# Layer 1's retention projection four columns ahead of the softmax attention instead of two

## The reference, cut to what matters

```python
pc = jnp.split(uc @ w_in, splits, axis=-1)
pl = jnp.split(ul @ w_in, splits, axis=-1)
...
b_c, b_l = _retention_branch(pc[1], pl[1], log_decay_raw, ret_norm_g, cos, sin, need_ctx)
c_c, c_l = _gqa_branch(pc[2], pl[2], qk_norm_g, cos, sin, need_ctx)
...
def _attend(q, k, v):
    s = jnp.einsum("bqkgd,bskd->bkgqs", q, k).astype(jnp.float32) * HEAD_DIM ** -0.5
    p = jax.nn.softmax(s, axis=-1).astype(v.dtype)
    return jnp.einsum("bkgqs,bskd->bqkgd", p, v)
```

## Time and profile before

| | before |
|---|---|
| median of 3 runs | 2147.62 us (2146.8 to 2147.97) |
| the profiled execution, its own time | 2146.09 us |
| span of its trace | 2144.2 us |
| PE busy | 2074.1 us, 97% of the span |
| DVE busy | 1568.4 us, 73% |
| ACT busy | 1150.0 us, 54% |
| POOL busy | 144.0 us, 7% |
| layer 1's retention columns and attention | from 1046.4 to 1109.0 us of the span |

### The profile page before, as it was taken

One profiled execution on the slowest core, in us unless ns is written; L12 is line 12 of the kernel. 1 busy time (PEld: TensorE's weight loads), 2 busy tenths in 40 slices (PEclk: granted clock), 3 DMA queues, 4 the chain that ended last, 5 costly groups with the idle time before them and its releaser, 6 DMA issues. The chain is left out here.

```text
span 2144.2 us, 36008 instructions
## 1 busy us (share of the span) xinstructions
PE 2074.1 (97%) x14750; PEld 1719.1 (80%) x14750; DVE 1568.4 (73%) x2201; ACT 1150.0 (54%) x1581; POOL 144.0 (7%) x118
## 2 busy tenths in 40 slices
PE   8999899999999999998998999999999999999997
PEld 5887687888888888877776899788888888888886
DVE  4546665889567555446466666699999999999998
ACT  4253443333432222244544355588888888888886
POOL 0013520000000000000045100100000000000000
PEclk9999999999999999999999999999999999999999
DMA  6700034454154545413000554599999999999995
GB/s 265 271 18 2 3 121 157 177 216 177 59 221 186 207 183 195 172 62 118 21 1 4 218 190 145 206 388 379 380 375 372 394 378 383 378 376 382 375 418 199
DMA packets 68485, 470.11 MB, mean 219 GB/s; under 512 B 7712, under 2 KB 8672, under 8 KB 14048
## 3 DMA queue, kind: packets, MB, share of 16 engines
q1 hardware_dynamic: 62464, 441.62, 53.5%
q10 hardware_dynamic: 4704, 21.98, 2.6%
q0 software_dynamic: 1152, 4.19, 0.5%
HBM read 455.15 MB, written 12.62 MB: 218 GB/s over the span
## 5 line engine op out<-in xcount | busy, mean ns | idle before, releaser
L2441 DVE TENSOR_TENSOR wsp_l<-ring,wsp_h 128x1024 fp32r<-128x1024 f32 x528 | 643.1, 1223 | 48.9 <-ACT wsp_h L1551 14.0
L1551 ACT CAST wsp_h<-ring 128x1024 fp32r<-128x1024 f32 x528 | 555.2, 1054 | 137.1 <-PE bank L719 81.2
L717 PE MATMUL bank<-wsp_h,xTs_h 128*128 128x512 f32 x704 | 283.7, 403 | 0.4 <-DVE wsp_l L2441 0.4
L719 PE MATMUL bank<-wsp_h,xTs_l 128*128 128x512 f32 x704 | 275.6, 391 | 0.0
L718 PE MATMUL bank<-wsp_l,xTs_h 128*128 128x512 f32 x704 | 274.4, 390 | 0.0
L2071 ACT CAST dsp_h<-ring 128x1024 fp32r<-128x1024 f32 x66 | 69.2, 1048 | 244.4 <-PE bank L1427 172.8
L3038 DVE TENSOR_TENSOR dsp_l<-ring,dsp_h 128x1024 fp32r<-128x1024 f32 x66 | 80.9, 1225 | 145.6 <-ACT dsp_h L2071 145.2
L1318 PE MATMUL bank<-u_hi,gsp_h 128*128 128x512 f32 (+1 forms) x512 | 174.1, 340 | 0.0
L1318 PE MATMUL bank<-u_hi,gsp_l 128*128 128x512 f32 (+1 forms) x512 | 172.1, 336 | 0.0
L1318 PE MATMUL bank<-x_lo,gsp_h 128*128 128x512 f32 (+1 forms) x512 | 172.0, 336 | 0.0
L2347 DVE SCALAR_TENSOR_TENSOR products<-ring,cond_rows 128x1024 bf16<-128x1024 f32 x128 | 156.4, 1222 | 5.0 <-DVE dsp_l L3038 0.5
(11 more groups left out here) (399 smaller groups left out, 4106.1 us busy)
## 6 DMA issues: line engine op xcount, KB each, us to landing
ring<-in_moe_tiles_dram SPq DMA_DIRECT2D x264, 1024.0 KB, 7.1
ring<-in_ada_tiles_dram SPq DMA_DIRECT2D x48, 1024.0 KB, 4.8
ring<-in_ffn_tiles_dram SPq DMA_DIRECT2D x33, 1024.0 KB, 6.8
ring<-in_gate_tiles_dram SPq DMA_DIRECT2D x32, 1024.0 KB, 6.8
ring<-in_in_tiles_dram SPq DMA_DIRECT2D x22, 1024.0 KB, 4.8
arena<-in_branch_tiles_dram ACTq DMA_DIRECT2D x8, 1024.0 KB, 7.4
ring<-in_out_tiles_dram SPq DMA_DIRECT2D x8, 1024.0 KB, 4.8
x_rows<-arena SPq DMA_DIRECT2D x1, 3584.0 KB, 15.9
```

The source lines that it names most:

```text
L717: pe.matmul(o, xTs[0][:, kk, :], whi[:, k, :], start=(kk == 0), stop=False)
L719: mm = pe.matmul(o, xTs[1][:, kk, :], whi[:, k, :], start=False, stop=(kk == KD - 1))
L1551: act.copy(wsp[0][:, g % 4, :], half_slot(MOE0, g)).then_inc(s.gq_o.up, 1)
L2441: v.tensor_tensor(wsp[1][:, g % 4, :], half_slot(MOE0, g), wsp[0][:, g % 4, :], ALU.subtract).then_inc(s.gq_pt.up, 1)
```

## The change

In layer 1 four columns stand ahead of the attention instead of two (`AHEAD`), as in layer 0. Column g is thus projected in step g-4 instead of g-2, and steps 8 and 9 have none. So that the weights are split in time, halves 16 and 17 are split before the transposes of the attention (ACT: around `root` and `fourier_out`; DVE: within its normalisation), halves 18 and 19 in the steps 0 and 1 (before: 1 and 2), halves 20 and 21 in the steps 3 and 4 (before: 5 and 6). The copies of PSUM follow the columns, and the copy after the loop is gone since its columns are now copied in step 7. Layer 0 is as it was.

```diff
-AHEAD = (4, 2)
+AHEAD = (4, 4)
...
                 ahead = AHEAD[l]
+                if l:
+                    weight_high(16)
                 root(small[:, 32:56], s.gq_sq, s.gq_rs)
                 fourier_out(0)
                 fourier_out(1)
-                weight_high(16)
+                if l == 0:
+                    weight_high(16)
+                else:
+                    weight_high(17)
...
-                weight_high(17)
+                if l == 0:
+                    weight_high(17)
...
-                    if n in (1, 2):
+                    if n in (1 - l, 2 - l):
                         act.wait_ge(*s.win_mm(UNITS + RDONE[l][0]))
-                        weight_high(17 + n)
+                        weight_high(17 + l + n)
                     if n % 2 and ahead + n < len(RCOLS[l]):
                         retention_evac((ahead + n) // 2)
-                    if n in (5, 6):
+                    if n in (5 - 2 * l, 6 - 2 * l):
                         act.wait_ge(*s.win_mm(UNITS + RDONE[l][1]))
-                        weight_high(15 + n)
+                        weight_high(15 + 2 * l + n)
...
                 else:
-                    retention_evac(RUNITS[l] - 1)
                     for t in range(NT):
                         rt_turn(t, t)
...
                 for t in (0, 2):
+                    if l:
+                        weight_low(16 + t // 2)
                     h0 = 0 if t in tiles else 4
...
                 v.wait_ge(*s.gq_tp(NT))
-                weight_low(16)
-                weight_low(17)
                 if l == 0:
+                    weight_low(16)
+                    weight_low(17)
                     v.wait_ge(*nil_out(32))
...
-                    if n in (1, 2):
-                        weight_low(17 + n)
-                    if n in (5, 6):
-                        weight_low(15 + n)
+                    if n in (1 - l, 2 - l):
+                        weight_low(17 + l + n)
+                    if n in (5 - 2 * l, 6 - 2 * l):
+                        weight_low(15 + 2 * l + n)
                     if n in (3, 4, 7, 8):
```

## The result

| | before | changed |
|---|---|---|
| median of 22 runs each | 2148.04 us | 2153.8 us |
| lowest and highest | 2144.64 to 2151.69 | 2146.3 to 2161.54 |
| ratio, 95% interval | | 1.0023, 1.0015 to 1.0031 |
| the profiled execution, its own time | 2146.09 us | 2161.54 us |

The medians differ by 5.8 us; the ratio of the runs, 1.0023, is 4.9 us, with 3.2 to 6.7 in its interval. The profiled execution of the changed kernel is its slowest run, so it shows more than the typical loss. Of the 15.5 us between the two profiled executions, 3.45 have been lost when column 0 begins (1049.85 instead of 1046.40), ahead of everything that the change can reach: the clock happened to fall in other places there.

The account below looks back on a forecast made before the run. PE, busy 97% of the span, was taken as the bound: +3.65 start, -3.1 clock, +3.7 stall, -1.2 tail make +3.0, plus 1.5 and 1.5 for low clock give +6.0, 2153.6 us; forecast 2151.5 to 2156, range 2148.2 to 2158.

Parts of the forecast that it names:

- The start: Ahead of layer 1's loop: two more columns hide the rotation's 2.82 us wait; scores of head 0 come 3.65 us later.
- The 3.1 us saved in the steps: Steps 0 to 7 without stalls: 40.3 us instead of 43.4, the difference being the price of the low clock.
- The stall in step 3: Late split and rotary step beside POOL in step 3 delay head 4's maximum; PE waits 3.7 us in step 5.
- The clock after the first gap: Low clock behind the 3.7 us idle stretch on PE: 1.5 us, between 0 and 3.1.
- The end: Steps 8 and 9, without columns: last rotary step still ends 7.4 us after step 7's column; PE idle 5.1 us.
- the tail: End of the loop: columns 10 and 11 and their copy no longer stand there, -1.2 us.
- The clock after the second gap: Low clock behind the 5.1 us idle stretch ahead of the retention's transposes: 1.5 us, between 0 and 3.1.
- the rival of a held clock: Rival: the stall in step 3 comes but the clock holds; +3.0 us, 2150.6 us, chance 0.15.
- Nothing behind absorbed the shift: After the retention's transposes: one chain to the program's end, no transfer or other engine absorbing a shift.

Follow-up runs that it names:

- the casts first: The changed kernel with ACT's casts of halves 20 and 21 ahead of the copy of PSUM in layer 1's steps 3 and 4; 2144.99 us, ratio 0.9997.
- changed_again: The changed kernel, nothing altered, run again on the other chip beside the kernel before; 2156.03 us against 2149.16, ratio 1.0036.

## Why the prediction came true, and where two errors cancelled

**The start** held: scores of head 0 predicted 3.65 us later, measured 14.06 - 10.55 = 3.51; the wait for the rotation gone, the clock at 1.00 up to step 5. The 3.1 us saved in the steps held as a sum too, but the prediction called all of it the price of the low clock. PE's wait of 1.08 us for the split of half 17, seen in the profile of idle products in the kernel before, lay hidden in it, and the change removes that wait as well, since the split now stands earlier.

**The stall in step 3** held in size and mechanism: predicted 3.7 us by copy, cast, split and a rotary step behind POOL's three instructions, measured 3.54. The casts first and the run without POOL's tables each took one link of the chain away, and the gap went in both. Filled with idle products, both waits kept their length.

**The clock after the first gap** was put at 1.5 us, from 0 to 3.1. Step 5, scores to scores, took 11.4 us: 5.3 + 3.54 + 2.6 for the clock; in the second profile 11.0, so 2.1. The term was a little too low. The low stretch is 6.8 us long in both; it begins 1.0 us before PE has work again in the first and 2.0 us before it in the second.

**The end** is the term that was mis-sized. I kept the 7.4 us from step 7's column to the end of the last rotary step. It took 1115.33 - 1110.43 = 4.9. The rotary step now starts 0.22 us ahead of POOL's first instruction, where before it started 0.40 after it, and its sixth instruction slips in at 1115.05, as POOL's long third starts at 1115.06. Before, its fifth was caught by the third, by the timeline of DVE:

```profile
1105.20 2.37 DVE L2399 TENSOR_TENSOR arena<-arena 128x128 f32<-128x128 f32 x1
```

That wait, some 2.1 us of these 2.37, was not there, and the whole rotary step took 3.2 us instead of 5.1. The working had seen that the two starts lie within some tenths of each other in step 3, but took over the old length for the end without asking which came first. The rotary step also started sooner after the column, 1.7 us instead of 2.3, since DVE was no longer behind. That POOL is met at all still costs 1.8 us against the 1.4 of a rotary step alone; some 1.2 us of the gap would stand without it (an estimate from these lengths). Predicted were -1.2 for the tail and a gap of 5.1 us, measured -3.5 (5.1 us from column to transposes instead of 8.6) and 2.97.

**The clock after the second gap** was put at 1.5 us, with 3.1 as the upper bound. From the retention's transposes to the decay products it takes 18.3 us at full clock (the kernel before), 19.5 with 3.4 us of low clock (the changed kernel again), 21.9 with some 10 (the casts first), and 23.8 with over 13 (the changed kernel): 1.2 to 5.6 us. The bound was wrong, since it took one low stretch of before for the longest that there is. The trace of the kernel before has one of over 13 us, outside the part that the prediction read:

```profile
961.00:974.00 13.00, 8.70 (x31) 6.86 (x32) 11.99 (x27) 10.20 (x23) 1.19 (x3) 0.50 0.19 81
```

In sum: without the clock behind the two gaps the change is worth +3.5 - 3.1 + 3.5 - 3.5 = +0.4 us, not +3.0; the kernel with idle products in both gaps bears this out with +0.6 at the decay products. That clock adds 3.4 (changed_again) to 8.2 us, not 3.0. The predicted +6.0 stands beside a measured 5.8 (4.9 by the ratio), but that is in part luck: the stall and the low clock came as forecast, while 2.6 us of the agreement are two errors of opposite sign, the tail too dear and the clock too cheap. The clock fell at both gaps in both profiles, so the rival of a held clock is out. Nothing behind absorbed the shift, as assumed: 3.9 us at the decay products of changed_again are 4.2 at its end. In the slowest run 3.4 us more were lost behind them, of which the profile shows only a further low stretch (6.8 us from 1211.5); whether the change has a part in it is not shown.

## What to carry to other kernels

Work that is moved forward takes its place in line with it: before a split, cast or copy goes to another step, ask what it stands behind on its own engine (here a copy that waits for the step's own column) and what stands behind it. Where VectorE and GpSimd share a phase, short instructions on VectorE with two operands in SBUF that another engine waits for belong in steps in which GpSimd is idle, or where nothing urgent follows; taking away one job of GpSimd can just move the next one up, as it did here. A gap of three microseconds on TensorE cost up to nearly twice that again in clock here (5.6 us behind one of 2.97), so two new gaps can undo a change that only moved idle time; and a gain at the start of a loop is kept only if the loop's last work has cover too, which is what moving the key's rotary steps gave (0.9977).

## What had not been expected

Gaps of nearly the same length, 2.97 to 2.98 us ahead of the same transposes, were followed by 3.4, about 10 and over 13 us at half clock, in three profiles. What sets the length is not shown. It is one reason why runs of one program differ: 2146.3 to 2161.54 us for the changed kernel, 2144.64 to 2151.69 for the one before. A single profile of such a kernel can be 8 us from its median; counted from a common instruction, two profiles agree to 0.05 us until the first low stretch.

Which of the two engines starts first decides, as finely as the records resolve it. A rotary instruction that DVE starts just ahead of POOL's is not held up (1115.05 beside 1115.06, 0.28 us long); one that starts 0.05 us behind it is, until POOL's ends (1085.98 beside 1085.93, 1.26 us long). Six short instructions against three long ones thus lost 1.8 us at the end (3.2 instead of 1.4), 3.7 before, and 4.0 in step 3.
